# One mixer's weight slabs reordered between its attention steps in a four-layer transformer kernel

## What is computed

```python
proj = h @ w_in                     # 1024 -> q, k, v, u, gate, 512 columns each
a_out = stick_breaking_attention(q, k, v)          # 8 heads of 64
c = u * jax.nn.sigmoid(gate)
c = causal_depthwise_conv(c, dw_w, dw_b)           # 31 taps, 512 channels
c = jax.nn.silu(layer_norm(c, ln_g, ln_b))
return jnp.concatenate([a_out, c], axis=-1) @ w_out
```

## Time and profile before

| what | value |
|---|---|
| median of 3 runs | 1807.41 us (1802.98 to 1809.21) |
| profiled execution, its own time | 1803.14 us |
| its span | 1801.4 us |
| mean granted TensorE clock | 0.973 of full |
| busy: PE, weight loads, DVE, ACT, POOL | 1684.7, 1566.7, 950.8, 847.8, 568.7 us |
| chain that ended last | PE 78%, DVE 12%, ACT 6% of the span |
| hybrid mixer, from its first slab to the end of its projection | 916.8 to about 1063 us |

### The profile page before, as it was taken

The page is one execution under the profiler, slowest core; times in us unless marked ns, Lnnn a source line. Parts: engine busy times, 40 slices in busy tenths (PEclk is TensorE's granted clock), DMA queues, the critical chain, the costliest instruction groups (busy, mean ns, idle before and its releaser), DMA issues.

```text
span 1801.4 us, 29175 instructions
## 1 busy us (share of the span) xinstructions
PE 1684.7 (94%) x11809; PEld 1566.7 (87%) x11818; DVE 950.8 (53%) x1399; ACT 847.8 (47%) x1137; POOL 568.7 (32%) x133
## 2 busy tenths in 40 slices
PE   7998999989999998999988589999999988899998
PEld 6997989979799997999977479998999978889997
DVE  1896685545666555533449854334533344654342
ACT  6323555543665555444454454445544454354443
POOL 5351223235613222223357103223222344503323
PEclk9999999989999998999999699999999998999999
DMA  8623765534245553554632215555455544415552
GB/s 263 196 71 110 131 227 191 182 117 141 79 132 182 191 204 111 195 186 167 233 129 94 94 47 190 196 186 187 149 190 186 188 144 150 140 64 194 175 191 89
DMA packets 220069, 283.50 MB, mean 157 GB/s; under 512 B 13004, under 2 KB 197315, under 8 KB 219987
## 3 DMA queue, kind: packets, MB, share of 16 engines
q1 hardware_dynamic: 216323, 276.08, 46.2%
q10 hardware_dynamic: 3664, 6.27, 1.8%
HBM read 280.88 MB, written 1.44 MB: 157 GB/s over the span
## 4 chain that ended last, share of the span: by engine, by line
PE 78%; DVE 12%; ACT 6%; issue 1%; DMA 1%; POOL 1%; ACTq 0%; DVEq 0%; SPq 0%
PE ps L1544 25%; PE ps L1545 24%; PE ps L1546 24%; DVE arena L1452 3%; PE ps L1791 2%; ACT w_hi L535 2%; DVE w_lo L1045 2%; ACT arena L566 1%; DVE x_lo L997 1%; DMA raw<-in_ffn_w_up 1%; DVE h L1031 1%; DVE xn L1026 1%; POOL w_lo L444 1%; DVE arena L1117 1%; ACT L560 1%
## 5 line engine op out<-in xcount | busy, mean ns | idle before, releaser
L444 POOL TENSOR_TENSOR w_lo<-raw,w_hi 128x2048 fp32r<-128x2048 f32 x117 | 552.7, 4738 | 1197.8 <-ACT w_hi L535 1197.8
L1544 PE MATMUL ps<-x_hi,w_hi 128*128 128x256 f32 (+1 forms) x2368 | 673.2, 284 | 8.6 <-DVE w_lo L1104 4.8
L1545 PE MATMUL ps<-x_lo,w_hi 128*128 128x256 f32 (+1 forms) x2368 | 671.3, 283 | 0.0
L1546 PE MATMUL ps<-x_hi,w_lo 128*128 128x256 f32 (+1 forms) x2368 | 671.2, 283 | 0.0
L535 ACT ACTIVATE w_hi<-raw 128x2048 fp32r<-128x2048 f32 x262 | 498.8, 1911 | 232.0 <-PE ps L1546 197.8
L1544 PEld LDWEIGHTS ps<-x_hi,w_hi 128*128 128x128 f32 (+1 forms) x2368 | 455.0, 192 | 15.0 <-issue 6.3
L1545 PEld LDWEIGHTS ps<-x_lo,w_hi 128*128 128x128 f32 (+1 forms) x2368 | 455.1, 192 | 2.2
L1546 PEld LDWEIGHTS ps<-x_hi,w_lo 128*128 128x128 f32 (+1 forms) x2368 | 454.9, 192 | 0.2
L1104 DVE TENSOR_TENSOR w_lo<-raw,w_hi 128x2048 fp32r<-128x2048 f32 x108 | 247.4, 2291 | 347.4 <-ACT w_hi L535 347.4
L1544 PE MATMUL ps<-w_hi,x_hi 128*128 128x256 f32 (+3 forms) x688 | 224.7, 327 | 25.1 <-DVE x_lo L997 14.4
L1545 PE MATMUL ps<-w_lo,x_hi 128*128 128x256 f32 (+3 forms) x688 | 218.7, 318 | 0.0
(11 more groups left out here) (172 smaller groups left out, 1431.1 us busy)
## 6 DMA issues: line engine op xcount, KB each, us to landing
raw<-in_ffn_w_in SPq DMA_DIRECT2D x88, 1024.0 KB, 5.1
raw<-in_ffn_w_up SPq DMA_DIRECT2D x44, 1024.0 KB, 5.2
raw<-in_ffn_w_out SPq DMA_DIRECT2D x44, 1024.0 KB, 4.9
raw<-in_ffn_w_down SPq DMA_DIRECT2D x22, 1024.0 KB, 4.9
raw<-in_hgrn_w_in SPq DMA_DIRECT2D x16, 1024.0 KB, 5.7
raw<-in_gla_w_in SPq DMA_DIRECT2D x12, 1024.0 KB, 5.5
raw<-in_hyb_w_in SPq DMA_DIRECT2D x10, 1024.0 KB, 5.1
raw<-in_dsa_w_in SPq DMA_DIRECT2D x6, 1024.0 KB, 5.3
```

Of the source, the lines that this page charges most:

```text
L444: pool.tensor_tensor(w_lo[slot][:, :], raw[slot][:, :], w_hi[slot][:, :].bitcast(F32), ALU.subtract)\
L1544: pe.matmul(out_ap, a_hi, b_hi, start=start, stop=False, skip_group_check=True)
L1545: pe.matmul(out_ap, a_hi, b_lo, start=False, stop=False, skip_group_check=True)
L1546: return pe.matmul(out_ap, a_lo, b_hi, start=False, stop=stop, skip_group_check=True)
```

## The change

- **Slab order** (`HYB_IN`): v0 and v1 first, then u0 gate0 q0 k0 u1 gate1 q1 k1. PE computes token block 0 of v0 and v1 (`half_token_slab`) before it turns block 1, and their block 1 later. The second half of the slabs stands between the attention steps of the first heads. q0 and k0 hold heads 0 to 3.
- **One slab early** (`EARLY_NEXT`): the third slab of the mixer (u0, slot 2) gets its high and its low at the end of the feed-forward layer before, ahead of the residual add.
- **Lows**: DVE makes 13 of the 14 lows of the mixer, POOL one (q0).
- **Convolution** in two halves: chunks 0 and 1 after u0 and gate0, chunks 2 and 3 after u1 and gate1. A tap waits for the tap two before it, no longer for that four before it.
- **Output projection** in two halves: k = 0 to 3 (heads) for both token blocks before the convolved channels are turned, k = 4 to 7 after them. The turn of block 0 of the next input comes after the projection, where it was inside it. The low parts of the heads are made before the last 26 taps.
- **ACT**: its list follows the new order; the Sqrt and Silu tables are loaded ahead of their use.

Left out of the diff below: the removed bodies of the old lists, code that only moved, and count keeping.

```diff
 WARM_NORMED = 8
 EACH = [slice(c, c + 1, 1) for c in range(NK)]
 PAIRS = [slice(c, c + 2, 1) for c in range(0, NK, 2)]
+HYB_IN = ((0, 4), (1, 5), (2, 6), (3, 8), (2, 0), (3, 2), (0, 7), (1, 9), (2, 1), (3, 3))
+EARLY_NEXT = (False, False, True, False, False, False)
...
             load_ffn(2)
-            load_four_columns(hyb_in, 6 * SLAB, 1)
-            load_four_columns(hyb_in, 0, 1)
-            for s in range(2):
-                load(s, [(raw_cols(s), col_slab(hyb_in, 4 * SLAB + s * SLAB))])
+            for s, col0 in HYB_IN:
+                load(s, [(raw_cols(s), col_slab(hyb_in, col0 * SLAB))])
...
             low_ffn(2)
-            ring.skip(0, 1)
-            ring.skip(1, 1)
-            for s in (2, 3, 0, 1, 2, 3, 0, 1, 2, 3, 0, 1):
-                low_one(s)
+            for s, n in ((0, 3), (1, 3), (2, 1), (3, 4)):
+                ring.skip(s, n)
+            low_one(2)
+            ring.skip(2, 2)
...
                 if f < len(FFNS) - 1:
                     high_one(d)
+                if EARLY_NEXT[f]:
+                    high_one(a)
...
+                    made[2] += 1
+                    high_one(2)
+                    sigmoid_gate(3, 0)
+                    high_one(3)
+                    for s in range(2):
+                        evacuate(s, hyb["v"][:, s, :], bank=s)
+                        high_one(s)
+                    evacuate(2, words(0, 512), bank=6)
+                    high_one(2)
+                    evacuate(3, words(1024, 512), 64 ** -0.5, bank=7)
+                    high_one(3)
+                    softplus_logs(0)
+                    softplus_logs(1)
                     made[0] += 1
-                    made[1] += 1
+                    sigmoid_gate(1, 1)
+                    stick_weights(0)
                     high_one(0)
                     high_one(1)
-                    for s in (2, 3):
...
-                    values_half(0)
-                    for pair in range(SB_HEADS // 2 + 1):
...
-                        .then_inc(cv_std, 1)
+                    evacuate(2, words(512, 512), bank=6)
+                    stick_weights(1)
+                    high_one(2)
+                    evacuate(3, words(1536, 512), 64 ** -0.5, bank=7)
+                    softplus_logs(2)
+                    softplus_logs(3)
+                    stick_weights(2)
+                    high_one(3)
+                    stick_weights(3)
                     act.wait_ge(sb_pv, SB_HEADS)
                     for b in range(2):
                         act.activation(x_hi[:, 2 * b:2 * b + 2, :].rearrange("p c t -> p (c t)"), ps[:, 4 + b, :], ACT.Copy)\
                             .then_inc(x_hi_done, 1)
+                    preload(ACT.Sqrt)
+                    act.wait_ge(cv_ms, 1)
+                    act.activation(ln_std, ln_mv.rearrange("p (b s) -> p b s", s=2)[:, :, 1], ACT.Sqrt, bias=eps_col)\
+                        .then_inc(cv_std, 1)
+                    preload(ACT.Silu, 155)
...
                     low_one(d)
+                if EARLY_NEXT[f]:
+                    low_one(a)
...
-                    taps = [(k, c) for k in range(CONV_TAPS) for c in range(CONV_CHUNKS)]
+                    lows.skip(2, 1)
...
+                            .then_inc(proj_free[u_slot], 1)
+                        dve.wait_ge(proj_free[u_slot], made[u_slot] + 1)
+
+                    last_tap = {}
+                    taps = [(k, 2 * half + c) for half in range(2) for k in range(CONV_TAPS) for c in range(2)]
...
                             src, dst, w = hyb["pad"][:, c, k:k + SEQ], hyb["co"][:, c, :], col("conv_dw_w_2", k * 4 + c)
+                            before = last_tap.get(c)
+                            last_tap[c] = want(cv_tap)
                             else:
-                                dve.wait_ge(cv_tap, want(cv_tap))
+                                dve.wait_ge(cv_tap, before)
...
 
-                    convolve(TAPS_AHEAD)
-                    for pair in range(SB_HEADS // 2):
-                        for hd in (2 * pair, 2 * pair + 1):
-                            stick_bound(hd)
-                        convolve(TAPS_BETWEEN)
-                        for hd in (2 * pair, 2 * pair + 1):
-                            stick_softplus(hd)
-                        convolve(TAPS_BETWEEN)
-                    assert not taps
...
+
+                    low_one(3)
+                    gated_half(0, 2, 3)
+                    convolve(3)
+                    low_one(3)
+                    convolve(2)
+                    low_one(0)
+                    low_one(1)
+                    convolve(9)
+                    low_one(2)
+                    convolve(7)
+                    bounds(0)
+                    low_one(3)
+                    convolve(6)
+                    softplus(0)
+                    convolve(5)
+                    bounds(1)
+                    convolve(12)
+                    softplus(1)
+                    for s in (0, 1):
+                        used[s] += 1
+                        made[s] += 1
+                    convolve(CONV_TAPS * 2 - (3 + 2 + 9 + 7 + 6 + 5 + 12))
+                    gated_half(1, 0, 1)
+                    low_one(0)
+                    low_one(1)
+                    convolve(16)
+                    low_one(2)
+                    bounds(2)
+                    convolve(6)
+                    bounds(3)
+                    softplus(2)
+                    convolve(6)
+                    softplus(3)
+                    low_one(3)
+                    convolve(8)
+                    low_of_banks(2)
+                    convolve(CONV_CHUNKS * CONV_TAPS)
+                    for s in (2, 3):
+                        used[s] += 2
+                        made[s] += 2
                     dve.wait_ge(cv_tap, CONV_CHUNKS * CONV_TAPS)
...
                                           ALU.subtract, ALU.mult).then_inc(cv_norm, 1)
-                    low_of_banks(2)
...
 
                 for tb in range(NTB):
-                    for k in range(NK):
+                    for k in ks:
...
@@ -1953,14 +2010,23 @@
                 turn_block(0)
                 if l == 0:
                     hyb = hyb_views()
-                    keep_warm(WARM_NORMED, 0)
-                    x_new()
-                    turn_after(1, x_new(0))
-                    project_four(feature_slab, 1, x_new())
-                    project_four(feature_slab, 1)
-                    project(token_slab, 0)
-                    for s in (2, 3):
-                        pe.wait_ge(proj_free[s], made[s] + 1)
+                    x0, x1 = x_new(), x_new()
+
+                    def slab_into(bank, s, fresh=None):
+                        begin(s)
+                        features(s, bank, 0, P, 0, fresh)
+                        features(s, bank, P, P, SEQ).then_inc(slab_used[s], 1)
+
+                    half_token_slab(0, 0, x0, 0)
+                    half_token_slab(1, 0, None, 1)
+                    turn_block(1)
+                    slab_into(4, 2, x1)
+                    slab_into(5, 3)
+                    half_token_slab(0, 1, None, 0)
+                    half_token_slab(1, 1, None, 1)
+                    slab_into(6, 2)
+                    slab_into(7, 3)
...
 
-                    for step in range(SB_HEADS // 2 + 2):
-                        if step < SB_HEADS // 2:
-                            stick_logits(2 * step)
-                            stick_logits(2 * step + 1)
-                        if step == 0:
-                            project(token_slab, 1)
-                        elif step < SB_HEADS // 2:
-                            keep_warm(WARM_STEP)
-                        if step == 2:
...
-                        if step == SB_HEADS // 2:
-                            conv_turned()
-                        if 1 <= step < SB_HEADS // 2 + 1:
-                            stick_rest(2 * step - 2)
-                            stick_rest(2 * step - 1)
-                        if step >= 2:
-                            stick_values(2 * step - 4)
-                            stick_values(2 * step - 3)
-
+
+                    heads(stick_logits, 0)
+                    slab_into(4, 0)
+                    heads(stick_logits, 1)
+                    slab_into(5, 1)
+                    heads(stick_rest, 0)
+                    slab_into(6, 2)
+                    for s in range(2):
+                        pe.wait_ge(proj_free[s], made[s] + 1)
+                    heads(stick_values, 0)
+                    heads(stick_rest, 1)
+                    slab_into(7, 3)
+                    all_copied()
+                    heads(stick_logits, 2)
+                    heads(stick_values, 1)
+                    heads(stick_logits, 3)
+                    keep_warm(2 * WARM_STEP)
+                    heads(stick_rest, 2)
+                    keep_warm(WARM_STEP)
+                    heads(stick_values, 2)
+                    heads(stick_rest, 3)
```

(12 more changed lines are left out.)

90 lines of the change are left out of this document (40 added, 50 removed).

## The result

The changed kernel takes 1789.78 us (median of 5 runs, 1785.17 to 1792.97), the kernel before 1807.41 (5 runs, 1802.98 to 1809.21): ratio 0.991 [0.988, 0.993], 17.6 us less. Timed a second time (experiment e10) it took 1791.32 against 1804.71: 0.992 [0.990, 0.994], 13.4 us less. The two pairs of medians put the gain at 13 and 18 us, and their intervals together allow 11 to 21. The forecast was 1788, from a sum with 17 us of gain.

A forecast was written before the change was run, and what follows sets the result against it. VectorE bounds the mixer behind the slabs, about 30 us of it exclusion with GpSimd. The next layer starts 17.7 us earlier, less 0.8: 1803.14 - 17 = 1786 us, 1790 by the median; 1788 was taken, range 1777 to 1800.

The forecast's parts named there:

- A: Rival: TensorE's clock stays low from 990 on and lists slip; gain only 6 to 12 us, 1793; chance 0.22.
- B: Rival: convolution taps, each waiting for the one two before, slow to a 0.59 us pace; 1810 us; chance 0.06.
- D: Rival: four ScalarE table switches cost more than their row, 5.1 us more on the path; 1791 us; chance 0.05.
- E: Rival: ScalarE's last output high and the logits come earlier, removing up to 7 us of VectorE waits; 1781; chance 0.10.
- behind the slabs VectorE is the bound: Mixer after the slab work: VectorE bounds it, with about 30 of its 88.6 us lost to exclusion with GpSimd.
- half slabs: TensorE's idle time before block 1's turn: two half slabs of v0 and v1 take 5.8 us, 911.3 to 917.1.
- The add at 904.3 ... Cost 2.0 us, on the path: Residual add ahead of the mixer: u0's early low delays it to 904.3, costing 2.0 us on TensorE's path.
- Waits ... 3.7 us: VectorE's second half: it waits 3.7 us for ScalarE's high of the last output slab, delaying the last tap.
- half of the 48 matmuls of block 0 are left, 6.0 us: Output projection after the turns back: only half of block 0's matmuls remain, 6.0 us, product ready at 1033.5.
- About 0.8 us: Next layer's start: TensorE restarts at the low clock after waiting, taking about 0.8 us off a 17.7 us gain.
- one low of GpSimd between 917 and 1070: Sign in the changed kernel's profile: GpSimd makes just one low between 917 and 1070.
- C: Rival: moved lows cost VectorE 20 us and list-order waits of 12 us more cancel the gain; 1803; chance 0.07.

The follow-up runs named there:

- e10: The changed kernel itself, unchanged, timed and profiled a second time: 1791.32 us, ratio 0.992 to the kernel before.
- e4: The kernel before with only the four output slabs' lows moved to VectorE, two behind each of the first two pairs' softplus: 1793.11 us, ratio 0.993.
- e1: The changed kernel with the four output slabs' lows made by GpSimd again: 1791.98 us, ratio 0.992 to the kernel before.
- e8: The changed kernel with u0's early low moved from ahead of block 0's residual add to ahead of block 1's split: 1788.56 us, ratio 0.992 to before.
- e11: e9 with the projection's first half started 8 taps earlier and the channels turned after 36 of its 48 matmuls, not 30: 1785.79 us, ratio 0.990 to before.
- e5: The changed kernel with v0 and v1 computed whole behind u0 and gate0, block 1 turned first: 1793.75 us, ratio 0.992 to the kernel before.
- e2: The changed kernel without the early slab, u0's high and low coming behind block 1's split: 1792.85 us, ratio 0.992 to the kernel before.
- e6: The changed kernel with the last output slab's high made earlier and 16 instead of 8 taps ahead of the heads' low parts: 1790.34 us, ratio 0.992 to before.
- e3: The changed kernel with the output projection in one piece behind the turns back, next block's turn inside it: 1792.54 us, ratio 0.993 to the kernel before.
- e7: e6 with the channels turned inside the projection's first half, without the eight matmuls of zeros: 1787.83 us, ratio 0.991 to the kernel before.
- e9: The changed kernel with the edits of e7 (which include those of e6) and e8 together: 1787.72 us, ratio 0.990 to the kernel before.

## Why the prediction was right

The sum said 1786 us for the profiled execution and 1790 for the median; they are 1788.66 and 1789.78. (The rivals' times are not all on one footing: A, B and D add to 1786, E takes from 1788.)

**The bound.** "behind the slabs VectorE is the bound", and 30 us of its 88.6 are the exclusion: right. Against one tap every 0.40 us the rows before have 28.6 us too much: 4.1 in the four first taps, 8.5 in the 60, 16.05 in the eight. e4 takes four lows from GpSimd to VectorE and does nothing else, and the 16.05 us go. e1 puts four back into the changed kernel, and 12.1 us of stalls return. The other 12.6 us were not taken away by themselves; in the changed kernel, where GpSimd's one low ends at 932.42 and the first tap starts at 932.95, no tap is long. That is 0.5 us to spare, and in e8 and e11 it is gone.

**The steps.** Forecast against the profile; its low of d starts 0.9 us ahead of that of before, so at the same distance a time would read 0.9 less:

| step | forecast | measured |
|---|---|---|
| start of the add (L1044) | 904.3 | 903.40 |
| half slabs | 911.3 to 917.1 | 910.37 to 918.06 |
| u0 starts | 919.5 | 919.73 |
| gate product of half 0 | 931.6 | 932.22 |
| VectorE's waits in its first half | 2.2 | 2.15 (0.44 + 0.57 + 0.93 + 0.21) |
| second gate product | 974.2 | 974.59 |
| low of the last output slab waits | 3.7 | 3.37 |
| last tap ends | 1018.1 | 1017.65 |
| projection, first half | 1007 to 1018-1019 | 1006.89 to 1018.04 |
| turns back | 1023.7 | 1022.74 |
| square of block 0's product | 1033.5 | 1033.91 |

The two half slabs start at the low clock (a matmul every 0.21 us, later every 0.12) and take 7.7 us, not 5.8. Not all of that fell into a time in which TensorE had nothing else: in e5, where they stand behind, u0 starts 2.06 us earlier (18.68 us behind the low of d for 20.74), and the prediction had put 0.7 us to it (919.5 for 916.84 + 2.0). The time behind the last tap was forecast as 15.4 us and is 16.26: the norm was 1.0 shorter, and the 24 matmuls of block 0 took 7.8 us for 6.0, since TensorE came out of 2.24 us without work and ran its first nine at the low clock (one every 0.43 us, then every 0.23). Such misses partly cancel, which is luck: the distance was forecast as 133.65 us (1033.5 - 899.85) and is 134.92.

**Mis-sized terms.** Besides these, two were right about the time and are not shown to be worth it:

- "The add at 904.3 ... Cost 2.0 us, on the path: TensorE waits for this chain." The delay of the add is 1.95 us (e2, the distance of the add from the low of d). Taking 1.5 us of it away alone (e8) moves the last tap by 1.55 and the end by 0.0, since TensorE's clock then falls in the projection's first half.
- "Waits ... 3.7 us" for the last high. The wait is there, and e6 removes it for 0.5 us. The prediction said that the projection's first half "is now late only together with" the taps, and drew no price from that sentence: TensorE's list is second by 0.2 us, and a gain on VectorE behind the heads' low parts is lost to it.

The projection in two halves had no term of its own in the sum; "half of the 48 matmuls of block 0 are left, 6.0 us" reads as 6 us gained, and e3 shows 1.6. "About 0.8 us" for a slower restart in the next layer did not show: from the add there (1036.87) to the next one but one (1238.51) are 201.6 us, 0.6 less than before. The sign "one low of GpSimd between 917 and 1070" was set too wide: the next layer's first one now starts at 1065.38.

**The rivals.** B (taps slow down): the pace is 0.40, 12 taps in 4.83 us, with each waiting for the one two before it; refuted. A (the clock): 0.96 and 0.95 from 985 to 1020, where it was 0.68; refuted in its size, not in its kind. The rest matmuls of pair 3 run at the low clock (3.42 us from their start to the zeros behind them, 1.86 in e8), which is hidden, since VectorE comes to the heads' low parts without a wait; block 0's last 24 cost 1.8 us on the path. A further 3.4 us were lost to the clock in another stage, which I had not looked at. D (table switches):

```profile
989.80 1.28 ACT L876 ACT_TABLE_LOAD   x1
991.10 0.94 ACT L876 ACTIVATE arena<-arena 128x384 f32<-128x384 f32 x2
992.05 1.28 ACT L873 ACT_TABLE_LOAD   x1
993.35 1.08 ACT L873 ACTIVATE arena<-arena 128x384 f32<-128x384 f32 x2
```

These are two of four switches in a row, each 1.28 us with 0.01 or 0.02 behind it; refuted. The Trainium skill (ScalarE: Activation LUTs, What ACT_TABLE_LOAD costs) has the load itself right; the 1.38 us of drain that it adds to a switch no row here shows, ahead of the load or behind it. C (nothing gained): waits of 12 us would have been needed; VectorE's two halves have 6.0. E (more): the last high and the logits came as forecast (waits of 3.37 us and of 0.20).

**What is shown and what isn't.** The single edits taken back cost 3.4 (e1), 5.1 (e2), 1.6 (e3) and 8.9 us (e5), 19.0 in all, more than the 16.45 of the whole, so they are no shares of a sum: each removes a wait that the others then expose, and some 4 us of them (1.0 in e2, 3.0 in e5) are TensorE's clock. That the exclusion is real and worth 11.2 us by itself in the kernel before is shown by e4; how the 16.45 us divide among the parts is not shown.

## What to carry to other kernels

Look in the timeline for rows whose mean length is several times that of the same instruction elsewhere, and for the engine that works just then: here one GpSimd operation of 4.6 us stopped one VectorE operation of 0.47 us, and moving four of them alone had two thirds of the whole gain. Before pricing a wait as lost time, ask which engine arrives second at the end of it and how much later: if it is 0.2 us, the wait is worth 0.2 us until that engine is made earlier too (e6 alone 0.5, with e7 3.6). Where an idle engine has spare work, let the step that the critical chain needs cut into it as soon as its input is there, and do the rest behind it (e7). And look at the clock before an edit is called worthless or good: in e8 and e9 it took back what the lists had gained.

## What the runs showed of the hardware

- VectorE and GpSimd keep each other out for whole instructions, both ways. A tap that meets a whole low takes 4.71 to 4.85 us for 0.47 (3.80 where the low was under way); a low issued in a row of taps at 969.01 ended at 984.81, 15.80 us for 4.6, and three take 16.50 us in e1, 13.8 alone. The Trainium skill (SBUF — State Buffer, SBUF: two separate sides) calls the shared port pair an exclusive lock, and the traces agree. Operations of VectorE that read one side from PSUM went on beside it: the heads' low parts in e1 take their usual 1.29 us from 1017.73, while GpSimd's fourth low runs from 1014.12 to 1018.63.
- A chain of taps in which each waits for the one two before it runs as fast as one without such a wait (0.40 us from start to start, with 0.47 us of length). Where each waits for the last, it is 0.59.
- TensorE's clock can fall at once after a wait or a little later. In the changed kernel, behind 2.24 us without work, all of the first nine matmuls start every 0.43 us; in e7, e9 and e11, behind 2.44 us, the first two or three run at the full clock (first one 0.47 us long) and then some eight are slow. In those TensorE had worked during most of the norm; in the changed kernel it had stood still for 2.10 us of it. Up to the square the difference is 7.63 against 7.33 to 7.36 us, so the earlier work was worth 0.3 us. What decides whether the clock falls (3.23 us without work bring it down in e5 and e8, not in e2) these runs don't show.
